# Cross attention's heads 1 to 3 and sliding attention's heads 1 to 7, one tick later

## What is computed

```
# delta rule, per head and chunk of 64
L   = where(strict, (k*beta) @ k.T * exp(diff), 0)
sol = solve(eye + L, [v*beta, k*beta*exp(gc)])      # u, w
# then a scan over 4 chunks: v_new = u - w S; o = q S + a v_new; S = d S + k v_new

# sliding window, 8 heads of width 64, blocks of 128 queries and up to 256 keys
p = softmax([q k / 8 masked, sink]);  y = p v * silu(z)

# cross attention, 4 heads of width 128
p = softmax(q mk / sqrt(128));        y = p mv * silu(z)

merged = sum_n sigmoid(gate_n) * (y_n @ w_up_n);  out = x + rmsnorm(merged @ w_out)
```

## Time and profile before

| | |
|---|---|
| median of 3 runs | 857.1 us |
| profiled execution | 858.77 us, its span 856.9 us |
| PE busy | 839.4 us (98%) |
| DVE busy, ACT busy | 625.2 us (73%), 510.1 us (60%) |
| POOL busy | 74.8 us (9%) |
| DMA | 148.45 MB, mean 173 GB/s |
| mean granted clock of PE | 0.997 of full speed |

### The profile page before, as it was taken

The page is one execution under the profiler, slowest core; times in us unless marked ns, Lnnn a source line. Parts: engine busy times, 40 slices in busy tenths (PEclk is TensorE's granted clock), DMA queues, the critical chain, the costliest instruction groups (busy, mean ns, idle before and its releaser), DMA issues. The chain is left out here.

```text
span 856.9 us, 14493 instructions
## 1 busy us (share of the span) xinstructions
PE 839.4 (98%) x5726; PEld 772.4 (90%) x5726; DVE 625.2 (73%) x1130; ACT 510.1 (60%) x839; POOL 74.8 (9%) x76
## 2 busy tenths in 40 slices
PE   8999999999999999999999899999999999999996
PEld 6999999999989999999999699999899888888885
DVE  5887987998877866666665868778745566776765
ACT  6665778665377756555666878754544443645453
POOL 0100002001020211111111200140000020000000
PEclk9999999999999999999999999999999999999999
DMA  8658443457455665655555365654433243355641
GB/s 290 234 171 292 151 148 121 147 202 293 145 178 187 223 202 175 196 178 193 172 196 172 129 216 170 238 159 150 147 103 118 78 140 103 120 201 195 197 148 49
DMA packets 40587, 148.45 MB, mean 173 GB/s; under 512 B 4652, under 2 KB 5320, under 8 KB 39880
## 3 DMA queue, kind: packets, MB, share of 16 engines
q1 hardware_dynamic: 40520, 147.54, 51.1%
HBM read 146.44 MB, written 1.08 MB: 172 GB/s over the span
## 5 line engine op out<-in xcount | busy, mean ns | idle before, releaser
L1872 DVE TENSOR_TENSOR t_wl<-t_raw,t_wh 128x1024 fp32r<-128x1024 f32 x258 | 313.7, 1225 | 102.4 <-ACT t_wh L1303 101.2
L1303 ACT ACTIVATE t_wh<-t_raw 128x1024 fp32r<-128x1024 f32 x258 | 270.9, 1059 | 107.7 <-PE bank L631 57.7
L629 PE MATMUL bank<-t_hh,t_wh 128*128 128x256 f32 x1136 | 327.9, 289 | 1.3 <-DVE t_wl L1872 1.2
L631 PE MATMUL bank<-t_hh,t_wl 128*128 128x256 f32 x1136 | 321.3, 283 | 0.0
L630 PE MATMUL bank<-t_hl,t_wh 128*128 128x256 f32 x1136 | 321.3, 283 | 0.0
L629 PEld LDWEIGHTS bank<-t_hh,t_wh 128*128 128x128 f32 x1136 | 217.6, 192 | 4.3 <-DVE t_wl L1872 2.0
L630 PEld LDWEIGHTS bank<-t_hl,t_wh 128*128 128x128 f32 x1136 | 217.7, 192 | 0.9
L631 PEld LDWEIGHTS bank<-t_hh,t_wl 128*128 128x128 f32 x1136 | 217.6, 192 | 0.0
L634 PE MATMUL bank<-t_wh,t_br 128*128 128x512 f32 x384 | 123.2, 392 | 0.0
L1887 DVE SCALAR_TENSOR_TENSOR t_arena<-bank,t_par,t_arena 128x255 f32<-128x255 f32 (+2 forms) x184 | 75.3, 475 | 45.4 <-ACT t_arena L1308 45.0
L634 PE MATMUL bank<-t_wh,t_hh 128*128 128x512 f32 x224 | 91.5, 408 | 3.2 <-DVE t_wl L1872 3.2
(11 more groups left out here) (151 smaller groups left out, 845.7 us busy)
## 6 DMA issues: line engine op xcount, KB each, us to landing
t_raw<-in_ws SPq DMA_DIRECT2D x258, 512.0 KB, 3.9
t_br<-decay SPq DMA_DIRECT2D x1, 2048.0 KB, 8.8
t_arena<-in_post SPq DMA_DIRECT2D x3, 512.0 KB, 5.1
t_arena<-gates SPq DMA_DIRECT2D x1, 1536.0 KB, 10.5
t_x<-in_xin SPq DMA_DIRECT2D x2, 512.0 KB, 4.8
t_bd<-in_bd SPq DMA_DIRECT2D x1, 1024.0 KB, 8.6
t_x<-in_xtok SPq DMA_DIRECT2D x1, 1024.0 KB, 6.5
t_arena<-in_mem SPq DMA_DIRECT2D x1, 1024.0 KB, 8.6
```

The source lines that it names most:

```text
L629: e.matmul(o, wh, xh, start=first, stop=False, skip_group_check=True)
L631: return e.matmul(o, wl, xh, start=False, stop=last, skip_group_check=True)
L1303: e.activation(WH[q % NS][:, :], RAW[q % NR][:, :], ACT.Copy, bias=0.0, scale=1.0).then_inc(*hi.now(q))
L1872: e.tensor_tensor(WL[q % NS][:, :], RAW[q % NR][:, :], WH[q % NS][:, :].bitcast(F), SUB).then_inc(*lo.now(q))
```

## The change

Ten rows of numbers move up by one: each tick of cross attention's heads 1 to 3 and of sliding attention's heads 1 to 7. Everything else, head 0 of both among it, stays where it is.

```diff
-T_XM = [(175, 177, 182), (183, 185, 186), (187, 189, 190), (191, 193, 194)]
-T_SW = [(179, 181, 190)] + [(191 + 4 * n, 193 + 4 * n, 194 + 4 * n) for n in range(7)]
+T_XM = [(175, 177, 182), (184, 186, 187), (188, 190, 191), (192, 194, 195)]
+T_SW = [(179, 181, 190)] + [(192 + 4 * n, 194 + 4 * n, 195 + 4 * n) for n in range(7)]
```

## The result

The change is slower: a median of 861.44 us (859.67 to 864.08, seven runs) beside 857.48 us (856.79 to 859.46, seven runs) of the kernel before. The ratio is 1.0046, 95% interval 1.0032 to 1.0059. The forecast was 855.3 us, with a range up to 857.0.

A forecast was written before the change was run, and what follows sets the result against it. PE, busy 98% of the span, bounds the kernel, so only its waits count. Terms −1.04 − 1.61 + 0.41 + 0.41 = −1.83 us from the 857.1 us median gave 855.3 us, range 854.2 to 857.0.

The forecast's parts named there:

- Tick 183, gain 1.04: Cross head 1 leaves 183 for 184, so ACT's copy comes before its exponential; PE's 1.04 us wait goes.
- tick 191, gain 1.61: Cross head 3 and sliding head 1 go to 192, behind no update; PE's 1.61 us wait for probabilities goes.
- Head 2's `y`, cost 0.41: Moved from tick 190 to 191, behind DVE's updates and masks; head 3's scores at 192 wait 0.41 us, bounds 0 to 1.5.
- Head 2's chain to 188, no cost: Cross head 2's softmax goes from 187 onto an update with masks; ACT's copy still in time by 2.7 us, cost nothing.
- rival 4: Head 2 at 188 holds ACT; PE waits at mid-190, then at 193, 2.2 us each: 859.7 us, chance 0.06.
- Rival 2: At tick 194 or elsewhere, PE waits 0.5 to 1.5 us for ACT's copy behind exponentials; with 1 us, 856.3; chance 0.27.
- Sliding head 2 to 196, cost 0.41: Its maximum stands behind spatial gating's low part on DVE; PE waits 0.41 us at tick 198, bounds 0 to 1.0.
- "All the other ticks", no cost: From 199 on, each moved head keeps two units, 5.7 us, against a chain of about 3.0; no gain or cost.
- The sum: Both gains and both new waits over the whole kernel, −1.83 us, giving 855.3 us, 0.21% less.
- The slower side, 0.08 for over 0.2%: Chance 0.08 that the whole kernel is slower by over 0.2%, from rival 4 and a bad form of Rival 2.

The follow-up runs named there:

- experiment 1: Cross attention's heads 1 to 3 one tick later, sliding attention as in the kernel before; 855.68 us, ratio 0.9976.
- experiment 4: Only cross attention's heads moved, as in experiment 1, plus DVE's second pair of masks taken at tick 192 instead of 191; 855.22 us, ratio 0.9973.
- experiments 5 and 6: ACT's exponentials of sliding head 2 at tick 197, behind the gate's tanh: on the whole change 859.21 us, on experiment 2 858.91 us.
- experiment 9: The whole change again with no edit, for a second profile; 861.47 us, ratio 1.0051 against the kernel before.
- experiment 2: Sliding attention's heads 1 to 7 one tick later, cross attention as in the kernel before; 862.46 us, ratio 1.0055.

## Why the prediction was wrong, point by point

- **Tick 183, gain 1.04, and tick 191, gain 1.61: right.** Both waits are gone, and experiment 1 has the gain alone, 0.24% less time.
- **Head 2's `y`, cost 0.41: right.** 1.22 us against 0.88, so 0.34; experiment 4 takes it away.
- **Head 2's chain to 188, no cost, and rival 4: right.** ACT does stand there, 6.35 us at `t_px` at 657.74, and PE doesn't wait. Rival 2 had the right mechanism, ACT blocked by an exponential ahead of a copy that PE wants, but at tick 194, where nothing happened. It counted a wait of this kind anywhere else as well, at a chance of 0.27 and at 0.5 to 1.5 us; it came at tick 196, and larger.
- **Sliding head 2 to 196, cost 0.41: here it failed.** The wait for `t_pw` exists (0.53 us in experiments 5 and 6), but the step followed only the chain's own result. ACT's exponentials wait for that chain too, and behind them stood a split and the tanh that frees a bank. The term was +2.74 instead of +0.41, and in two of three profiles a fall of the clock worth 1.7 us came with it.
- **"All the other ticks", no cost: failed at tick 212.** The margin of two units was that of each head's own chain. The delta rule's first output stands at 212, and behind the two DVE should have emptied a projection's bank: +1.53 us.
- **The sum.** It was −1.83; with the two terms corrected it is +2.0, against +2.64 between the landmarks, whose last 0.6 us no term had; where the clock falls, its 1.7 us bring that to +4.3. The runs measured +3.9 and +4.4. The prediction had bounded the term at 196 by 1.0 us "if ACT does not come to the exponential at once". That was the wrong thing to bound: not how late ACT comes to the exponential matters, but how long it is held there, and what follows it in the queue.
- **The range and the chances.** The slower side, 0.08 for over 0.2%, hung on rival 4's one place, tick 188, and a bad form of rival 2. The same mechanism at ten moved rows deserved a look at each place where a moved chain meets a lane that stays.

## What to carry to other kernels

When a waiting instruction is moved in an in-order queue, follow two lists: who waits for its result, and what stands behind it in the same queue and whom that serves. Here the first was worth 0.3 us, with another 0.5 hidden, and the second 4.3 us, and PSUM banks that the moved work doesn't use were the link. A table that is shifted as a whole should be tried part by part first: one half of this one, run alone, gained 0.24%, the other cost 0.55%.

## What the runs showed of the hardware

A wait of 2.6 us in the middle of dense matmuls was in two of three profiles followed by a fall of PE's granted clock from full speed to 0.50, 1.2 GHz, for some microseconds, at a price of 1.7 us in the windows of experiment 9. PE had been busy without a gap up to that wait (6.00 of 6.00 us from 690 to 696 in experiment 2). The waits of 1.4 us (before at 677 us, after at 763 us) never did this in the profiles taken here. The Trainium skill (TensorE: Matmul & The Clock Gate, Part 1: The HAM clock gate) says that the gate follows how busy PE has been recently. The windows of experiments 2 and 9 agree: the clock is 1.00 up to the wait and lower behind it. The first profile of the change shows that it isn't certain: the same program with the same wait kept 1.00 there.

That does not explain the whole scatter of the change. Its slowest execution, 864.08 us, is the profiled one in which the clock did not fall behind the wait; it was late from the start, at the first landmark 4.2 us behind experiment 9's (584.33 against 580.16).
